# Where the split weights begin in SBUF: the rings of high and low weight parts start 16 bytes further on

## What is computed

```python
def conv_glu_ffn(h, w_gate, w_up, conv_w, conv_b, w_down):        # twice
    g = causal_dwconv(h @ w_gate, conv_w) + conv_b
    return (jax.nn.silu(g) * (h @ w_up)) @ w_down

def swiglu(h, w_gate, w_up, w_down):                              # four times
    return (jax.nn.silu(h @ w_gate) * (h @ w_up)) @ w_down

x = x + even_mixer(rmsnorm(x, ...), ...)   # h @ w_in, convolutions, @ w_out
x = x + odd_mixer(rmsnorm(x, ...), ...)    # h @ w_in, recurrence, attention, @ w_out
x = x + 0.5 * g1[:, None, :] * swiglu(h, ffn1_w_gate[l], ffn1_w_up[l], ffn1_w_down[l])
```

## Time and profile before

| | us |
|---|---|
| median of 3 runs | 1564.45 (1564.17 to 1564.61) |
| the profiled execution | 1564.03 |
| its span, first to last instruction | 1562.1 |
| PE busy | 1541.1 (99%) |
| DVE busy | 1253.9 (80%) |
| ACT busy | 847.9 (54%) |
| chain that ended last, on PE | 83% |
| chain that ended last, on DVE | 10% |

### The profile page before, as it was taken

How to read it: one execution, slowest core, us unless ns; L and a number is a source line. 1 busy time by engine, 2 the same in 40 slices (tenths; PEclk the granted TensorE clock), 3 DMA queues, 4 the chain that set the end, 5 groups by cost and what they waited for, 6 DMA issues and landing times.

```text
span 1562.1 us, 26739 instructions
## 1 busy us (share of the span) xinstructions
PE 1541.1 (99%) x10894; PEld 1430.3 (92%) x10894; DVE 1253.9 (80%) x1588; ACT 847.9 (54%) x1014; POOL 52.2 (3%) x61
## 2 busy tenths in 40 slices
PE   9999999999999999999999999999999999999998
PEld 7989999998799999999999999999999999999997
DVE  7988899787578998978878797887888888785555
ACT  6666555664466545744446664445644456564443
POOL 1000000100010000000000010000000000100000
PEclk9999999999999999999999999999999999999999
DMA  7605887453247885488863359886598854355551
GB/s 298 205 34 178 329 305 251 177 185 136 75 140 295 309 291 186 170 331 314 314 226 139 115 198 322 316 310 225 199 329 306 309 172 163 135 190 188 188 188 68
DMA packets 59805, 344.11 MB, mean 220 GB/s; under 512 B 6800, under 2 KB 7312, under 8 KB 28752
## 3 DMA queue, kind: packets, MB, share of 16 engines
q1 hardware_dynamic: 58752, 340.80, 61.4%
q0 software_dynamic: 544, 1.97, 0.3%
q10 hardware_dynamic: 432, 0.27, 0.1%
HBM read 341.96 MB, written 1.05 MB: 220 GB/s over the span
## 4 chain that ended last, share of the span: by engine, by line
PE 83%; DVE 10%; ACT 3%; issue 3%; DMA 1%; SPq 0%; ACTq 0%; DVEq 0%
PE PS L680 26%; PE PS L768 23%; PE PS L683 13%; PE PS L670 7%; PE PS L648 5%; PE PS L737 3%; DVE wl L1475 3%; PE PS L657 2%; DVE Z L1818 2%; DVE XL L1494 1%; PE PS L819 1%; DMA raw<-weights 1%; ACT wh L1037 1%; DVE RS L1507 1%; PE PS L844 1%
## 5 line engine op out<-in xcount | busy, mean ns | idle before, releaser
L1475 DVE TENSOR_TENSOR wl<-raw,wh 128x2048 fp32r<-128x2048 f32 (+2 forms) x256 | 569.7, 2229 | 131.6 <-ACT wh L1037 129.8
L1037 ACT ACTIVATE wh<-raw 128x2048 fp32r<-128x2048 f32 (+2 forms) x256 | 475.4, 1859 | 130.8 <-PE PS L768 107.7
L680 PE MATMUL PS<-HP,wh 128*128 128x512 f32 x1728 | 542.7, 395 | 0.0
L683 PEld LDWEIGHTS PS<-HP,wl 128*128 128x128 f32 x1728 | 324.6, 188 | 76.8
L683 PE MATMUL PS<-HP,wl 128*128 128x256 f32 x1728 | 339.6, 278 | 0.0
L768 PE MATMUL PS<-FX,wh 128*128 128x256 f32 x1920 | 309.7, 281 | 0.0
L768 PEld LDWEIGHTS PS<-FX,wh 128*128 128x128 f32 x1920 | 265.0, 190 | 0.0
L680 PEld LDWEIGHTS PS<-HP,wh 128*128 128x128 f32 x1728 | 263.4, 189 | 0.0
L768 PE MATMUL PS<-FX,wl 128*128 128x256 f32 x960 | 199.4, 281 | 0.0
L1574 DVE SCALAR_TENSOR_TENSOR ada<-ada,AR 128x1024 f32<-128x1024 f32 x144 | 172.8, 1219 | 0.0
L768 PEld LDWEIGHTS PS<-FX,wl 128*128 128x128 f32 x960 | 151.5, 190 | 0.0
(11 more groups left out here) (274 smaller groups left out, 1676.7 us busy)
## 6 DMA issues: line engine op xcount, KB each, us to landing
raw<-weights SPq DMA_DIRECT2D x242, 1024.0 KB, 5.1
ada<-ada_w SPq DMA_DIRECT2D x144, 512.0 KB, 6.3
raw<-weights SPq DMA_DIRECT2D x6, 768.0 KB, 4.4
raw<-weights SPq DMA_DIRECT2D x4, 576.0 KB, 4.8
X<-x SPq DMA_DIRECT2D x2, 512.0 KB, 5.7
raw<-weights SPq DMA_DIRECT2D x2, 512.0 KB, 6.9
out<-Z SPq DMA_DIRECT2D x4, 256.0 KB, 2.4
AR<-c POOLq DMA_DIRECT2D x1, 512.0 KB, 8.1
```

Of the source, the lines that this page charges most:

```text
L680: mm(pairs(bank(bk + m)), lhsT=lhs(0, k, m * P), rhs=HP[:, k], start=k == 0, stop=False, skip_group_check=True)
L683: last = mm(bank(bk + m, 0, S), lhsT=lhs(1, k, m * P), rhs=HH[:, k, :], start=False, stop=k == k_tiles - 1, skip_group_check=True)
L1037: last = A_(dst(wh), src, ACT.Copy)
L1475: last = tt(dst(wl), src, dst(wh).bitcast(F32), ALU.subtract)
```

## The change

Both rings become one tensor, which is 32 numbers (128 bytes) longer than the two were. The first 4 numbers (16 bytes) are left free, `wh` and `wl` follow one behind the other, and 28 numbers are left free behind them.

```diff
+SKEW = 4
...
         raw = sb("raw", [P, RAW, UNIT])
-        wh = sb("wh", [P, SPL, UNIT], F32R)
-        wl = sb("wl", [P, SPL, UNIT], F32R)
+        split = sb("split", [P, SKEW + 2 * SPL * UNIT + 28], F32R)[:, SKEW:SKEW + 2 * SPL * UNIT].rearrange(
+            "p (h i u) -> p h i u", h=2, u=UNIT)
+        wh, wl = split[:, 0], split[:, 1]
         ada = sb("ada", [P, ADA_RING, D])
```

## The result

The changed kernel takes 1569.39 us (median of 8 runs, 1569.16 to 1569.67), the kernel before beside it 1564.49: a ratio of 1.0030, 95% interval 1.0021 to 1.0039. It is slower by some 5 us. The forecast was 1558.6 and faster; the time lies in the range, on the other side of no change.

A forecast was written before the change was run, and what follows sets the result against it. PE's matmul count times start distance was taken to bound the kernel. Terms of -7.0 and +1.2 us gave -5.8 on the profiled 1564.03, so 1558.2, and 1558.6 for the median; range 1547 to 1576.

The forecast's parts named there:

- What bounds the kernel: PE, busy 99% of the span: time is the number of matmuls times the distance between their starts.
- Place matters, by the distance: Matmul pace follows the moving operand's offset from the ring weights: 119.8 ns at 0, 117.7 at 64.
- No effect: Rival: pace depends on the moving operand's own place, not its distance from the weights; 1564.4 us, chance 0.23 including cancelling effects.
- Distance modulo 128: Offsets of all products with ring weights were counted modulo 128, making the change a step of -16.
- The 16 bytes as a place like any other, at -1.05 ns: Some 6650 matmuls going from offset 0 to 112 gain 1.05 ns each, -7.0 us (ends -14.0 and +14.0).
- `XH`: 1184 matmuls streaming from this tensor keep a mix of offsets: 0 us (ends -1 and +1).
- `paired`: Feed-forward units of 512- and 256-column matmuls, 1728 + 1728, given the same -1.05 ns a matmul.
- Mixers against `HP`: Mixer units streaming from this tensor at offset 0, about 120 ns a matmul, were to gain 1.05 ns each.
- Odd blocks: The 30 odd down blocks, 1440 matmuls at offset 0: 5.75 us for 48 becomes 5.70 or less.
- Offset 64: About 2320 matmuls, including even down blocks, going to 48 lose 0.5 ns each: +1.2 us (ends 0 and +4.9).
- Slower: Rival: at -16 the stream meets the weight load badly, offsets 0 and 64 each pay +2.1 ns; 1583 us, chance 0.25.
- Much faster: Rival: the skew removes the whole meeting of load and stream, up to 11 ns a matmul; -112 us, 1453, chance 0.07.

The follow-up runs named there:

- e4: Against the kernel before, only the low weights' ring begins 16 bytes further on, and all behind it 128; 1568.8 us, ratio 1.0029.
- e5: Against the kernel before, rings stay and 128 free bytes are added behind them, moving everything behind; 1556.6 us, ratio 0.9952.
- e1: Against the kernel before, rings and all behind them begin 32 bytes further on, every distance kept; 1564.3 us, ratio 0.9999.
- e11: Against the kernel before, rings and every tensor streamed against them begin 16 bytes further on, distances kept; 1562.2 us, ratio 0.9987.
- e13: The changed kernel's distances modulo 256, but with rings as in the kernel before and moving tensors 16 bytes off a multiple of 32; 1555.7 us, ratio 0.9945.
- e3: Against the kernel before, rings begin 64 bytes further on and all behind them 128; 1552.0 us, ratio 0.9921.

## Why the prediction was wrong

**What bounds the kernel: right.** PE's matmul distance carries the difference (+5.9 us by the starts, +5.5 in the span). DVE's subtraction (2229 ns on average over all its forms, the same mean as on the page of before) and ACT's copy did not get slower with the new begin, which the prediction had costed at nothing, and the clock stayed full but for 3 of the first 14 us.

**Place matters, by the distance: right in kind.** "No effect" falls: e4 and e5 have the moving operands in the same places and differ by 12.1 us, and e1 shows that moving both operands alike by 32 bytes does nothing. The Trainium skill ("TensorE: Matmul & The Clock Gate", Part 2, the step LDWEIGHTS) says that loading the next weights takes no read bandwidth from the running matmul. The traces show that the place of the weights matters to the running matmul all the same: 113.3 to 120.0 ns for the same 256 columns. Whether that is bandwidth or something else they do not show. Nor is it the distance alone (e11, e13).

**Distance modulo 128: a step that failed, and hid a gain.** The prediction counted places modulo 128, so that the 128 bytes by which everything behind the rings moved were nothing, and the change was a step of -16. e5 has those 128 bytes alone and gains 7.8 us. The distances did not go from 0 to -16 and from 64 to 48, but from 0 to 112 and from 64 to 176 modulo 256. The argument that a stream passes every place modulo 128 eight times had been noted and led nowhere; that two tensors at the same place modulo 128 had the same pace (odd blocks and `HP` at 119.8) fitted 256 as well, since both happened to be at 0 there. This step did not turn the sign: with the 128 bytes alone the kernel takes 1556.6, close to the 1558.6 forecast, but for another reason.

**The 16 bytes as a place like any other, at -1.05 ns: the step that turned the sign.** The bounds of the forecast came from rows in which nothing began off a multiple of 32 bytes but rows of `XH`, and weights never did. On top of the 128 bytes, the 16 bytes ahead of the rings cost 12.8 us (e5 to after), and ahead of the low ring alone 12.1 (e4). With the rings there and the operands not, the changed kernel loses 13.7 us to e13 at the same distances.

**Term by term.** `paired`, forecast -1.05 x 3456 = -3.6 us, measured +5.4: 9.0 of the 10.8 us between forecast and result lie here. Carrying a pace from 256-column matmuls of the down units to `paired` had no row behind it, and it was the largest term. Its sign differs from that of the odd blocks, at the same distance, in the same kernel. Mixers against `HP`: forecast -1.05, measured -0.2 a matmul, 1.5 us. Odd blocks: forecast -1.05, measured -1.4. Offset 64: forecast +0.5 a matmul, measured +0.8 to +1.0, and the last blocks more: +2.4 us where +1.2 stood. `XH`: 0, measured +0.4. That the odd blocks came near is luck and no support for the reasoning, since they are a mean of two paces, 116.7 and 119.8 to 120.0.

Two small slips in the sum: 168 of its 6650 matmuls stream the weights against `HP`, so their offset went to +16 and not to 112 (at most 0.4 us); and "slower" needed not 0.9 but some 0.3 ns over offset 0, as (3 - 1.2) / 6650 gives, to be told from no change.

**The rivals.** "Slower" had the sign, and a quarter of the chance, but not the mechanism: it held that all offsets near the weights' lose alike, while odd blocks gained. "Much faster" (1453) is refuted as far as it was tried: the best distance found, 192, takes 6.5 of the 13 ns in the 256-column matmuls, and 0.7 to 0.9 of the 14 in `paired`.

**What would show it.** The page and the chain sorted this as it was laid out: odd blocks forecast at 5.70 (5.76 and 5.60), even at 5.66 to 5.70 (5.70), the piece between at 11.09 (11.26), and a unit against `HP` below 0.36 us for three, as the first shown, at 5.75 for 48, is not. The sign named as the one that refutes the forecast, `paired` going with the slower kind, is what came.

**What stays open**: why the rings at 16 modulo 32 cost with operands on multiples of 32 and not in e11; what the remaining excess of some 6.6 ns at the best distance is; and why the fp32 products, at 429 ns for 1024 cycles, show next to none of it.

## What to carry to other kernels

In this kernel, where float32r matmuls with a weight load each stand back to back, the distance between moving operand and weights in SBUF, modulo 256 bytes, is a tuning knob worth up to 6.7 ns of 120 a matmul of 256 columns; measure it for each pair of tensors by putting free bytes between them, and do not move the weights alone off a multiple of 32 without a measurement. When an edit puts free bytes into a chain of tensors, list everything that moves behind them, and do not assume a period that the trace has not shown. A pace measured on one shape of stream is a guess for another: the largest term of a sum deserves a row of its own.

## What the runs showed that was not expected

The same block, at the same addresses, can run at one of two steady paces. After has odd blocks at 119.8 and 116.7 ns in turn, e3 at 117.8 and 113.3, and e11 has pairs of `paired` units at 175.0 and at 173.3 ns in one feed-forward. The kernel before has it in the last blocks of its feed-forwards, all at distance 64: 113.4 in two of them, 117.8 or 117.9 in four. Four of the five odd blocks of a feed-forward are the same instructions, run in a loop on the same slots. In the chain of e11, feed-forward 0, the odd blocks 1, 3 and 5, of which the middle one is faster:

```profile
162.21 5.68 PE PS L771 x48
...
195.87 5.60 PE PS L771 x48
...
229.44 5.68 PE PS L771 x48
```

The order of paces repeats in most feed-forwards of a run. It would fit that the place allows more than one rhythm and that what came before picks one; no run shows it. A mean over a group, such as the 118.4 of the odd blocks after, need not be a pace that any block has.
